# Two blocks on one NeuronCore: the order of VectorE's work in the key and state-space stage, and small matmuls placed in more tiles of the array

## The chip, the cores and the metric

The kernel runs on one NeuronCore of one Trainium2 chip. The number is the time of one execution on the device in microseconds (us), less being better. The program is written by hand for five engines: TensorE multiplies matrices, VectorE and ScalarE work on rows of 128 partitions, GpSimd and SyncE start transfers. Each engine executes its own list of instructions strictly in the order in which it is written, and waits at semaphores for the others.

## The reference

Two transformer blocks with a sequence of 512 and a width of 1024, batch 1, all in float32. The change lies in the first of them:

```python
ssm_u, ssm_z, q, k, v, attn_z, q_idx, k_idx, w_idx = jnp.split(h @ w_in[l], split_points, axis=-1)
# state-space mixer: 32 groups of 16 channels, 64 complex states in each
bu = jnp.einsum('gpc,bsgc->bsgp', b_bar, ug)
_, states = lax.associative_scan(_ssm_combine, (a_seq, bu), axis=1)
y = jnp.einsum('gcp,bsgp->bsgc', c_mat, states).real + d_skip * uf
z = jax.nn.gelu(y); z = z * jax.nn.sigmoid(z @ w_glu + b_glu)
# sparse attention: 8 heads of 64, every query keeps its 128 best keys
k = rms_norm(k.reshape(bsz, seq, N_HEADS, HEAD_DIM), k_gain)
score = jnp.einsum('bqh,bqhs->bqs', wib, jax.nn.relu(rel))
_, sel = lax.top_k(score, 128)
p = jax.nn.softmax(jnp.einsum('bqhd,bqkhd->bqhk', qb, k_sel) * scale + bias)
```

The second block (retention, gated linear attention, window attention, feed-forward) is the longer part of the time and is not touched.

## The kernel before

Large products are computed in float32 precision from two fp32r parts: every weight tile (1024 x 256) is loaded by SyncE, ScalarE casts it to its high part (`split_high`, L1211), VectorE subtracts to get the low part (`split_low`, L1852), and TensorE does three matmuls for each 128 rows (`gemm_half`). A tile is two halves; a half takes 24 matmuls of 512 columns, or 48 of 256 for the value tiles. `w_low` is the semaphore that says that a tile's low part is there.

The stage of the change comes after the query tiles. TensorE's list is: second half of the first key tile; `key_stats` (sums of squares of the keys by head); `output_strip(0)`; the two halves of the second key tile and the halves of the first value tile, with a `key_stats` and an `output_strip` behind each of the first three; the first half of the second value tile; four matmuls that spread the inverse norms of the keys over partitions (`kr_psum`); the last value half; two small products for the gate; the 16 steps of state-space outputs (`y_psum`); transposes; the GLU product; and then the attention's logits, which need the keys, the values, and `z_ready`, `mod_ready` and `copied_dve`, the last of VectorE's signals in this stage.

`output_strip` computes, for each of 16 pairs j of groups and each of the two groups r in it, a strip of 16 x 128 numbers from the state matrices: contraction over 64 rows, 16 output rows. Four pairs make a strip q. ScalarE copies strip q out of PSUM with `strip_copy(q)` in two instructions. VectorE adds the skip term to all strips (`diag`, L2170), which needs the semaphore `strip_act` at 8, that is all four copies; GpSimd then spreads them into `toep` with eight DMAs, which TensorE's outputs read.

ScalarE's list here is: `head_chunk` (copy and square of a quarter of the keys, behind the half that computed it), `strip_copy(0)`, the cast of the first value tile, the third head chunk, `strip_copy(1)`, the fourth head chunk, `strip_copy(2)`, the cast of the second value tile, `strip_copy(3)`, the root of the key sums.

VectorE has three kinds of work: the low parts of the weights; `states(0)` and `states(1)`, each the rotations and scans of half of the pairs; and the selection of keys. `select_keys(n)` is n rounds, each of which finds the 8 largest scores of a row (L2095) and strikes them out (L2096). 48 rounds are needed, 16 for each of three query tiles, on 256, 384 and 512 scores; they may lie anywhere before the attention reads the masks, so the program spreads them by hand.

Of the kernel before, what the change touches and what calls it, by code (L numbers as in the profile page):

```python
# [19 lines left out]
P = 128  # L20
# [9 lines left out]
STEPS = 8  # L30
# [131 lines left out]
def hybrid_blocks(nc, wstream, xT, vecs, consts, head_rows, onehot, rel_bias, ssm_vec, ssm_b, ssm_c, d_skip,  # L162
# [13 lines left out]
    with ctx:  # L176
# [124 lines left out]
        cl_zero, bias_spread = sem("cl_zero"), sem("bias_spread")  # L301
        ki_copied, ki_doubled, wi_ready, wi_row, wi_psum, mod_row, gate_row = sem("ki_copied"), sem("ki_doubled"), sem("wi_ready"), sem("wi_row"), sem("wi_psum"), sem("mod_row"), sem("gate_row")
# [250 lines left out]
        def _(pe):  # L553
# [207 lines left out]
            def key_stats(c):  # L761

                s0 = SQ0["k"]
                pe.wait_ge(sq_ready, s0 + c + 1)
                mm(bank[3][0:HEADS, :], head_cols[:, c, :], sqb[:, (s0 + c) % 2, :], c == 0, c == 3)\
                    .then_inc(sq_used, 1)
# [33 lines left out]
            def output_strip(q):  # L800

                if q:
                    pe.wait_ge(strip_act, 2 * q)
                for i in range(4):
                    j = 4 * q + i
                    for r in range(2):
                        rows = slice(64 * r, 64 * r + 64)
                        out = bank[5 + r][0:GCH, i * P:i * P + P]
                        mm(out, bb_re[rows, j, :], cl_re[rows, j, 0:P], True, False)
                        ins = mm(out, bb_im[rows, j, :], cl_im[rows, j, 0:P], False, True)  # L810
                ins.then_inc(strip_psum, 1)
# [3 lines left out]
            output_strip(0)  # L815
# [3 lines left out]
            output_strip(1)  # L819
            gemm_half(gr, 1, "fm", h_hi, h_lo)  # L820
            key_stats(2)
            output_strip(2)
            gemm_half(G["v"][0], 0, "tm", h_hi, h_lo)
            key_stats(3)
            output_strip(3)
            gemm_half(G["v"][0], 1, "tm", h_hi, h_lo)
            gemm_half(G["v"][1], 0, "tm", h_hi, h_lo)
            pe.wait_ge(rstd_ready, ROOT["k"] + 1)
# [13 lines left out]
            for q in range(4):  # L842
                if q >= 2:
                    pe.wait_ge(y_act, 2 * q - 2)
                for i in range(4):
                    j = 4 * q + i
                    outs = [bank[4 + 2 * (q % 2) + r][0:64, i * P:i * P + P] for r in range(2)]
# [345 lines left out]
        def _(act):  # L1193
# [175 lines left out]
            def strip_copy(q):  # L1369

                act.wait_ge(strip_psum, q + 1)
                for r in range(2):
                    act.copy(strip[:, 8 * q + r:8 * q + 8:2, :],
                             bank[5 + r][0:GCH, :].rearrange("p (i c) -> p i c", c=P)).then_inc(strip_act, 1)
# [11 lines left out]
            act.activation(root[0:HEADS, :], bank[3][0:HEADS, :], ACT.Sqrt, bias=eps[0:HEADS, 0:1],  # L1386
                           scale=1.0 / 64).then_inc(root_ready, 1)
            for w, gr in enumerate(G["v"]):
                if w == 0:
                    evacuate_tm(gr, 0, v32[:, 0:2, 0:WC])  # L1390
                    evacuate_tm(gr, 1, v32[:, 2:4, 0:WC])
                    continue
# [1376 lines left out]
```

## Time and profile before

| | |
|---|---|
| Time, median of 3 runs | 1565.63 us (1564.47 to 1566.12) |
| The profiled execution: its own time | 1562.42 us |
| The profiled execution: span from first to last instruction | 1560.4 us |
| TensorE busy | 1489.6 us, 95% of the span |
| VectorE busy | 857.8 us, 55% |
| ScalarE busy | 601.4 us, 39% |
| Mean granted TensorE clock | 0.980 of full speed |

The span is one slice of the whole: the stage of the change lies between 158 and 271 us of it. A row of a timeline gives the start, the duration, the engine, the line of the program (a helper's, so many operations share L555 or L1809), what is written and read, how many instructions are merged in the row, and in brackets the idle time before it with what ended it. A float32 matmul appears as two instructions.

### The profile page before, as it was taken

To read this page: it belongs to the slowest core of one execution; us is meant where nothing else is said; L and a number is where in the kernel's file an instruction comes from. 1 tells how busy PE (TensorE), PEld (TensorE's weight loads), DVE (VectorE), ACT (ScalarE), POOL (GpSimd) and SP (SyncE) were. 2 spreads that over 40 slices of the span, in tenths; PEclk is the share of its full clock that TensorE was granted. 3 is DMA by queue.
4 is the path that set the end of the run, shared out by engine and by line. 5 is a ranking of instruction groups with operands and counts; after the bars stand their busy time and mean duration, and the time that the engine had idled before them with its cause. 6 is when DMAs were issued, how large, how long until landed. Compare 5 with 4: busy or idle time off the path is not lost.

```text
span 1560.4 us, 19534 instructions
## 1 busy us (share of the span) xinstructions
PE 1489.6 (95%) x7920; PEld 1196.7 (77%) x7920; DVE 857.8 (55%) x1445; ACT 601.4 (39%) x912; POOL 20.7 (1%) x36
## 2 busy tenths in 40 slices
PE   4799998999999999999999999999997999999997
PEld 1575786667887788888888877888886888888886
DVE  5889797785636664333426444433447644444234
ACT  3334515565324654333426434432333322222220
POOL 0011010000000000000000000000000000000000
PEclk8799999999999999999999999999998999999998
DMA  8523254105331211212222212222231232322221
GB/s 320 184 86 80 80 126 149 55 1 189 135 108 57 79 55 55 81 59 81 112 98 91 81 55 81 81 84 105 102 141 70 93 107 83 109 83 100 102 95 55
DMA packets 24472, 152.39 MB, mean 98 GB/s; under 512 B 3472, under 2 KB 6080, under 8 KB 8112
## 3 DMA queue, kind: packets, MB, share of 16 engines
q1 hardware_dynamic: 21872, 137.43, 24.3%
q0 software_dynamic: 2512, 13.72, 3.2%
q8 instruction: 63, 1.03, 0.3%
q14 instruction: 25, 0.20, 0.0%
HBM read 144.55 MB, written 7.88 MB: 98 GB/s over the span
## 4 chain that ended last, share of the span: by engine, by line
PE 86%; DVE 9%; ACT 2%; issue 1%; DMA 1%; SPq 0%; DVEq 0%; ACTq 0%
PE bank L555 84%; DVE score L2115 1%; DMA xr<-xT 1%; PE bank L962 1%; ACT w_hi L1211 1%; DVE score L2096 1%; DVE w_lo L1852 1%; DVE small L2095 1%; PE bank L894 0%; DVE sv L1809 0%; DVE rstd L1883 0%; DVE w_lo L1861 0%; DVE tval L2059 0%; DVE y_lo L1878 0%; DVE rstd L1924 0%
## 5 line engine op out<-in xcount | busy, mean ns | idle before, releaser
L555 PE MATMUL bank<-h_hi,w_hi 128*128 128x512 f32 (+1 forms) x1104 | 441.0, 399 | 12.6 <-DVE h_lo L2618 7.8
L555 PE MATMUL bank<-h_hi,w_lo 128*128 128x512 f32 (+1 forms) x1120 | 438.7, 392 | 0.0
L555 PE MATMUL bank<-h_lo,w_hi 128*128 128x512 f32 (+1 forms) x1104 | 432.2, 391 | 0.0
L1852 DVE TENSOR_TENSOR w_lo<-w_raw,w_hi 128x2048 fp32r<-128x2048 f32 (+2 forms) x106 | 239.2, 2257 | 256.9 <-ACT w_hi L1211 255.4
L555 PEld LDWEIGHTS bank<-h_hi,w_hi 128*128 128x128 f32 (+1 forms) x1104 | 208.1, 188 | 70.5 <-issue 22.2
L1211 ACT CAST w_hi<-w_raw 128x2048 fp32r<-128x2048 f32 (+2 forms) x109 | 204.5, 1876 | 138.7 <-PE bank L555 135.8
L555 PEld LDWEIGHTS bank<-h_hi,w_lo 128*128 128x128 f32 (+1 forms) x1120 | 211.1, 188 | 45.8 <-issue 0.9
L555 PEld LDWEIGHTS bank<-h_lo,w_hi 128*128 128x128 f32 (+1 forms) x1104 | 208.3, 189 | 42.4 <-issue 1.2
L555 PE MATMUL bank<-y_hi,w_hi 128*128 128x512 f32 x272 | 109.8, 404 | 4.6 <-DVE y_lo L1878 4.6
L555 PE MATMUL bank<-y_lo,w_hi 128*128 128x512 f32 x272 | 106.8, 393 | 0.0
L555 PE MATMUL bank<-y_hi,w_lo 128*128 128x512 f32 x272 | 106.8, 393 | 0.0
L555 PE MATMUL bank<-w_hi,h_hi 128*128 128x256 f32 x352 | 102.0, 290 | 0.0
L555 PE MATMUL bank<-w_hi,h_lo 128*128 128x256 f32 x352 | 100.3, 285 | 0.0
L555 PE MATMUL bank<-w_lo,h_hi 128*128 128x256 f32 x352 | 100.2, 285 | 0.0
L1558 ACT ACTIVATE sgb<-bank 128x512 f32<-128x512 f32 x40 | 23.9, 598 | 150.9 <-PE bank L555 150.9
L555 PE MATMUL bank<-f_hi,w_lo 128*128 128x512 f32 (+1 forms) x220 | 76.2, 347 | 0.0
L555 PEld LDWEIGHTS bank<-w_hi,h_hi 128*128 128x128 f32 x352 | 68.2, 194 | 7.3 <-issue 7.3
L555 PE MATMUL bank<-f_hi,w_hi 128*128 128x512 f32 (+1 forms) x196 | 69.7, 356 | 0.0
L555 PE MATMUL bank<-f_lo,w_hi 128*128 128x512 f32 (+1 forms) x196 | 69.4, 354 | 0.0
L555 PEld LDWEIGHTS bank<-w_lo,h_hi 128*128 128x128 f32 x352 | 68.2, 194 | 0.0
L555 PEld LDWEIGHTS bank<-w_hi,h_lo 128*128 128x128 f32 x352 | 68.2, 194 | 0.0
L555 PEld LDWEIGHTS bank<-y_hi,w_hi 128*128 128x128 f32 x272 | 51.6, 190 | 18.9 <-issue 5.7
(382 smaller groups left out, 1826.3 us busy)
## 6 DMA issues: line engine op xcount, KB each, us to landing
w_raw<-wstream SPq DMA_DIRECT2D x120, 1024.0 KB, 4.8
xr<-xT SPq DMA_DIRECT2D x2, 2048.0 KB, 11.1
w_raw<-wstream SPq DMA_DIRECT2D x4, 768.0 KB, 4.1
bias_rows<-bias_table POOLq DMA_DIRECT2D x1, 2560.0 KB, 12.2
bias<-bias_rows POOLq DMA_DIRECT2D x1, 2048.0 KB, 11.9
x_saved<-xr POOLq DMA_DIRECT2D x1, 2048.0 KB, 9.9
xr<-x_saved POOLq DMA_DIRECT2D x1, 2048.0 KB, 8.0
outT<-down SPq DMA_DIRECT2D x16, 128.0 KB, 1.8
```

The costliest lines, as they stand in the source:

```text
L555: return pe.matmul(out, lhsT, rhs, start=start, stop=stop)
L962: ins = pe.transpose(bank[ST_BANKS[t % 2]][:, j * P:j * P + P], lg[:, n % 2, j, kb * P:kb * P + P], ident)
L1211: act.copy(hi_of(s)[:, 0:kt, :], w_raw[:, i % RAW_SLOTS, 0:kt, :]).then_inc(w_high, 1)
L1558: act.activation(sgb[:, m % 2, :], bank[bk][:, :], func).then_inc(bank_free[bk], 1)
L1852: dve.tensor_tensor(w_low_of(s)[:, 0:kt, :], w_raw[:, i % RAW_SLOTS, 0:kt, :], hi_of(s)[:, 0:kt, :].bitcast(f32), ALU.subtract).then_inc(w ...
L2095: settle(dve.max(m8, s))
L2096: settle(dve.match_replace(s, m8, s, NEG_TAKEN))
L2115: dve.scalar_tensor_tensor(out=score[:, qt, 0:w], in0=sgb[:, i % 2, 0:w], scalar=wi[:, qt, h:h + 1], in1=score[:, qt, 0:w], op0=ALU.mult, ...
```

## The change

- `output_strip(q)`, four calls, becomes `output_strips()`, one call behind the first `key_stats`: strip q goes to PSUM partitions 32q to 32q + 15, so that the four q and the two r use eight tiles of the array; the loop over q and r is inside. `strip_copy(q)` stays where it was in ScalarE's list and waits for the one signal.
- The state-space outputs of group r go to PSUM partitions 64r to 64r + 63 (before, 0 to 63 for both).
- `key_stats` computes the sums by tokens: 128 partitions of tokens by 2 heads, four small matmuls for each quarter, as the queries' sums already are. ScalarE's root and VectorE's reciprocal then work on 128 x 32 instead of 8 x 512. A new `key_rows()` on TensorE transposes the result to 8 x 512 before the second value tile, and ScalarE copies it out (`kr_row`).
- On VectorE, six rounds stand before the wait for the query roots, none before `states(0)`; the skip term on the strips stands before `states(1)` instead of behind it; the 8 rounds behind `states(1)` are gone; the reciprocal of the key roots comes right behind `states(1)`, then the low part of the second value tile, then 5 rounds. Further on it is 12, 8 and three times 3 rounds instead of 14, 9 and three times 1. The number of rounds is 48 in both.

```diff
             def key_stats(c):
                 s0 = SQ0["k"]
                 pe.wait_ge(sq_ready, s0 + c + 1)
-                mm(bank[3][0:HEADS, :], head_cols[:, c, :], sqb[:, (s0 + c) % 2, :], c == 0, c == 3)\
-                    .then_inc(sq_used, 1)
+                for t in range(TT):
+                    ins = mm(bank[3][:, t * HEADS + 2 * c:t * HEADS + 2 * c + 2],
+                             sqb[:, (s0 + c) % 2, t * P:t * P + P], head_ones[:, 0:P:64], True, True)
+                ins.then_inc(sq_used, 1)
+
+            def key_rows():
+                pe.wait_ge(rstd_ready, ROOT["k"] + 1)
+                for t in range(TT):
+                    ins = pe.transpose(bank[3][0:HEADS, t * P:t * P + P], stat[:, 0, t * HEADS:(t + 1) * HEADS], ident)
+                ins.then_inc(kr_turned, 1)
...
-            def output_strip(q):
-                if q:
-                    pe.wait_ge(strip_act, 2 * q)
+            def output_strips():
                 for i in range(4):
-                    j = 4 * q + i
-                    for r in range(2):
-                        rows = slice(64 * r, 64 * r + 64)
-                        out = bank[5 + r][0:GCH, i * P:i * P + P]
-                        mm(out, bb_re[rows, j, :], cl_re[rows, j, 0:P], True, False)
-                        ins = mm(out, bb_im[rows, j, :], cl_im[rows, j, 0:P], False, True)
+                    for part in range(2):
+                        bb, cl = ((bb_re, cl_re), (bb_im, cl_im))[part]
+                        for q in range(4):
+                            for r in range(2):
+                                rows = slice(64 * r, 64 * r + 64)
+                                out = bank[5 + r][32 * q:32 * q + GCH, i * P:i * P + P]
+                                ins = mm(out, bb[rows, 4 * q + i, :], cl[rows, 4 * q + i, 0:P], part == 0, part == 1)
                 ins.then_inc(strip_psum, 1)
...
-            output_strip(0)
+            output_strips()
             gr = G["k"][1]
             gemm_half(gr, 0, "fm", h_hi, h_lo)
             key_stats(1)
-            output_strip(1)
             gemm_half(gr, 1, "fm", h_hi, h_lo)
             key_stats(2)
-            output_strip(2)
             gemm_half(G["v"][0], 0, "tm", h_hi, h_lo)
             key_stats(3)
-            output_strip(3)
             gemm_half(G["v"][0], 1, "tm", h_hi, h_lo)
+            key_rows()
             gemm_half(G["v"][1], 0, "tm", h_hi, h_lo)
-            pe.wait_ge(rstd_ready, ROOT["k"] + 1)
+            pe.wait_ge(kr_row, 1)
...
-                    outs = [bank[4 + 2 * (q % 2) + r][0:64, i * P:i * P + P] for r in range(2)]
+                    outs = [bank[4 + 2 * (q % 2) + r][64 * r:64 * r + 64, i * P:i * P + P] for r in range(2)]
...
             stt(qg[:, :], v("q_gain", 0), -0.125, v("k_gain", 0), ALU.mult, ALU.mult)
+            select_keys(6)
             dve.wait_ge(root_ready, ROOT["q"] + 1)
...
             split_low(8)
-            select_keys(4)
             states(0)
             split_low(9)
-            states(1)
-            settle(dve.memset(ga_[:, :, 0:1], 0.0))
-            dve.memset(gb_[:, :, 0:1], 0.0).then_inc(state_ready, 1)
-            select_keys(8)
-            split_low(10)
             dve.wait_ge(strip_act, 8)
...
             dve.wait_ge(strip_ready, 1)
+            states(1)
+            settle(dve.memset(ga_[:, :, 0:1], 0.0))
+            dve.memset(gb_[:, :, 0:1], 0.0).then_inc(state_ready, 1)
             dve.wait_ge(root_ready, ROOT["k"] + 1)
-            dve.reciprocal(rstd[0:HEADS, :], root[0:HEADS, :]).then_inc(rstd_ready, 1)
-            select_keys(2)
+            dve.reciprocal(stat[:, 0, :], stat[:, 0, :]).then_inc(rstd_ready, 1)
+            split_low(10)
+            select_keys(5)
...
-            select_keys(14)
+            select_keys(12)
             split_low(G["glu"][0].s)
-            select_keys(9)
+            select_keys(8)
...
                     if m < 3:
-                        select_keys(1)
+                        select_keys(3)
```

On VectorE, around the skip term of the strips (`strip<-strip,tval`; `w_lo` is a low part, MAX and MATCH_REPLACE a round), the kernel before has:

```order
L2095 MAX small<-score 128x8 [waits dve_step]
L2096 MATCH_REPLACE score<-small,score 128x256 [waits dve_step]
L1852 TENSOR_TENSOR w_lo<-w_raw,w_hi 128x2048 [waits w_high,dve_step]
L1809 TENSOR_TENSOR tval<-cst,small 16x512 [waits strip_act]
L2170 TENSOR_TENSOR strip<-strip,tval 16x32x16 [waits dve_step]
L2173 RECIPROCAL rstd<-root 8x512 [waits root_ready,strip_ready]
```

and the changed kernel has, behind the first half of the states (`gb_`) and before the second (`tval<-ga_,cos_t`):

```order
L1818 TENSOR_TENSOR gb_<-gb_,tval 128x8x63 [waits dve_step]
L1861 TENSOR_TENSOR w_lo<-w_raw,w_hi 128x2048 [waits w_high,dve_step]
L1818 TENSOR_TENSOR tval<-cst,small 16x512 [waits strip_act]
L2174 TENSOR_TENSOR strip<-strip,tval 16x32x16 [waits dve_step]
L1818 TENSOR_TENSOR tval<-ga_,cos_t 128x512 [waits x_act,strip_ready]
L1818 TENSOR_TENSOR tval<-gb_,sin_t 128x512 [waits dve_step]
```

The instruction that waits for `strip_act` has moved ahead of `states(1)` and of the rounds, and everything of VectorE that follows is queued behind it.

Behind the second half of the states, the changed kernel has on VectorE:

```order
L1818 TENSOR_TENSOR gb_<-gb_,tval 128x8x63 [waits dve_step]
L2177 MEMSET ga_ 128x16 [waits dve_step]
L2178 MEMSET gb_ 128x16 [waits dve_step]
L2180 RECIPROCAL stat<-stat 128x32 [waits root_ready]
L1861 TENSOR_TENSOR w_lo<-w_raw,w_hi 128x2048 [waits w_high]
L2104 MAX small<-score 128x8
L2105 MATCH_REPLACE score<-small,score 128x256 [waits dve_step]
```

The reciprocal of the key roots, now on 128 x 32, and the low part of the second value tile stand directly behind `states(1)`; before, 8 rounds lay between.

On TensorE, the strips (`bb_re`, `bb_im` with `cl_re`, `cl_im`) behind the first sums of the keys read, before:

```order
L555 MATMUL bank<-h_hi,w_lo 128x512
L555 MATMUL bank<-sqb,cst 8x512
L555 MATMUL bank<-cl_re,bb_re 16x128
L555 MATMUL bank<-cl_im,bb_im 16x128
L555 MATMUL bank<-cl_re,bb_re 16x128
```

and now:

```order
L556 MATMUL bank<-h_hi,w_lo 128x512
L556 MATMUL bank<-cst,sqb 128x2 x4
L556 MATMUL bank<-cl_re,bb_re 16x128 x8
L556 MATMUL bank<-cl_im,bb_im 16x128 x8
L556 MATMUL bank<-cl_re,bb_re 16x128 x8
```

The real parts of all eight tiles of an i come first, then the imaginary ones, and the strips no longer alternate with key and value tiles.

Later on TensorE, between the two value tiles, there is now:

```order
L556 MATMUL bank1<-w_hi,h_lo 128x256
L775 MATMUL bank3<-cst,stat 8x128 [waits rstd_ready]
L775 MATMUL bank3<-cst,stat 8x128 x3
L556 MATMUL bank2<-w_hi,h_hi 128x256 [waits w_low,bank_free2]
L556 MATMUL bank2<-w_lo,h_hi 128x256
```

The transposes of the key roots (`cst,stat`) wait for VectorE's reciprocal, and the value tile behind them (`w_hi,h_hi` into bank 2) for its low part; nothing of TensorE's list can pass them.

## Rows read from the trace of the kernel before

**Rows 1.** The page, part 4: shares of the span on the chain that ended last

```profile
PE 86%; DVE 9%; ACT 2%; issue 1%; DMA 1%; SPq 0%; DVEq 0%; ACTq 0%
```

**Rows 2.** Timeline of VectorE, 163 to 184: start us, us, operation, [idle before]

```profile
163.89 0.35 DVE L2131 RECIPROCAL stat<-stat 128x32 f32<-128x32 f32 x1 [5.33 <-ACT stat L1357]
...
167.82 0.42 DVE L2095 MAX8 small<-score 128x8 f32<-128x256 f32 x1
...
168.79 0.43 DVE L2095 MAX8 small<-score 128x8 f32<-128x256 f32 x1
...
171.74 0.69 DVE L1809 TENSOR_TENSOR tval<-ga_,cos_t 128x512 f32<-128x512 f32 x1
...
183.47 2.29 DVE L1852 TENSOR_TENSOR w_lo<-w_raw,w_hi 128x2048 fp32r<-128x2048 f32 x1
```

**Rows 3.** Timeline of TensorE, 174 to 183, first strip and the half behind it

```profile
174.48 0.40 PE L555 MATMUL bank<-cl_re,bb_re 64*16 64x128 f32 x4
...
176.34 0.50 PE L555 MATMUL bank<-h_hi,w_hi 128*128 128x512 f32 x1
...
182.02 1.02 PE L555 MATMUL bank<-sqb,cst 128*8 128x512 f32 x2
```

**Rows 4.** TensorE's groups by form, 163 to 250: xcount | busy us, mean ns

```profile
L555 PE MATMUL bank<-ut,win_re 128*64 128x64 f32 x64 | 2.3, 223 | 0.5 <-ACT stat L1357 0.5
```

**Rows 5.** Timeline of ScalarE, 191 to 204

```profile
191.23 0.60 ACT L1225 ACTIVATE sqb<-bank 128x512 f32<-128x512 f32 x1
...
194.41 1.91 ACT L1211 CAST w_hi<-w_raw 128x2048 fp32r<-128x2048 f32 x1
...
202.21 1.05 ACT L1373 COPY strip<-bank 16x512 f32<-16x512 f32 x2 [5.90 <-PE bank L555]
```

**Rows 6.** Timeline of VectorE, 207 to 215, strips, key roots, keys

```profile
207.63 0.67 DVE L1809 TENSOR_TENSOR tval<-cst,small 16x512 f32<-16x512 f32 x1
...
209.04 3.34 DVE L2173 RECIPROCAL rstd<-root 8x512 f32<-8x512 f32 x1
...
215.03 3.25 DVE L2177 SCALAR_TENSOR_TENSOR k<-k,qg,bank 128x512 f32<-128x512 f32 x4 [0.29 <-PE bank L555]
```

**Rows 7.** Timeline of TensorE, 207 to 228: last value tile, start of the outputs

```profile
207.95 0.28 PE L555 MATMUL bank<-w_hi,h_hi 128*128 128x256 f32 x1
...
213.80 3.70 PE L555 MATMUL bank<-rstd,sgb 8*128 8x512 f32 x8
...
226.74 0.43 PE L555 MATMUL bank<-cl_re,ga_ 64*64 64x128 f32 x4
...
227.32 0.65 PE L555 MATMUL bank<-toep,ut 128*64 128x128 f32 x4
...
227.90 0.43 PE L555 MATMUL bank<-cl_re,ga_ 64*64 64x128 f32 x4
```

**Rows 8.** Timeline of VectorE, 238 to 256

```profile
238.27 1.23 DVE L1852 TENSOR_TENSOR w_lo<-w_raw,w_hi 128x1024 fp32r<-128x1024 f32 x1 [2.49 <-ACT w_hi L1211]
...
242.30 0.69 DVE L2095 MAX8 small<-score 128x8 f32<-128x512 f32 x1
...
243.81 0.69 DVE L2095 MAX8 small<-score 128x8 f32<-128x512 f32 x1
...
253.06 2.50 DVE L1878 TENSOR_TENSOR y_lo<-z,y_hi 128x512 fp32r<-128x512 f32 x4 [0.17 <-DVE score L2096]
```

**Rows 9.** Timeline of TensorE, the three longest waits in question

```profile
253.90 0.77 PE L555 MATMUL bank<-y_hi,w_hi 128*128 128x512 f32 x1 [3.10 <-DVE y_lo L1878]
...
270.56 0.49 PE L555 MATMUL bank<-k,q 64*128 64x128 f32 x4 [2.29 <-DVEq L2201]
...
1181.75 0.77 PE L555 MATMUL bank<-h_hi,w_hi 128*128 128x512 f32 x1 [7.82 <-DVE h_lo L2618]
...
1187.01 0.47 PE L555 MATMUL bank<-h_hi,w_hi 128*128 128x512 f32 x1
```

**Rows 10.** Windows: PE busy, PEld, DVE, ACT, POOL, then the granted clock

```profile
1182.00:1186.00 4.00, 4.00 (x10) 3.17 (x11) 3.93 (x7) 2.38 (x5) 0.00 (x0) 0.50 0.00 0
```

More of the change, by code:

```diff
@@ L301, in hybrid_blocks @@
         cl_zero, bias_spread = sem("cl_zero"), sem("bias_spread")
+        kr_turned, kr_row = sem("kr_turned"), sem("kr_row")
         ki_copied, ki_doubled, wi_ready, wi_row, wi_psum, mod_row, gate_row = sem("ki_copied"), sem("ki_doubled"), sem("wi_ready"), sem("wi_row"), sem("wi_psum"), sem("mod_row"), sem("gate_row")
@@ L1369, in strip_copy @@
             def strip_copy(q):
-                act.wait_ge(strip_psum, q + 1)
+                act.wait_ge(strip_psum, 1)
                 for r in range(2):
                     act.copy(strip[:, 8 * q + r:8 * q + 8:2, :],
-                             bank[5 + r][0:GCH, :].rearrange("p (i c) -> p i c", c=P)).then_inc(strip_act, 1)
+                             bank[5 + r][32 * q:32 * q + GCH, :].rearrange("p (i c) -> p i c", c=P)).then_inc(strip_act, 1)
             strip_copy(0)
@@ L1385, in _ @@
             act.wait_ge(rstd_ready, ROOT["k"])
-            act.activation(root[0:HEADS, :], bank[3][0:HEADS, :], ACT.Sqrt, bias=eps[0:HEADS, 0:1],
+            act.activation(stat[:, 0, :], bank[3][:, 0:32], ACT.Sqrt, bias=eps[:, 0:1],
                            scale=1.0 / 64).then_inc(root_ready, 1)
@@ L1391, in _ @@
                     evacuate_tm(gr, 1, v32[:, 2:4, 0:WC])
+                    act.wait_ge(kr_turned, 1)
+                    act.copy(rstd[0:HEADS, :], bank[3][0:HEADS, :]).then_inc(kr_row, 1)
                     continue
@@ L1413, in _ @@
                              u[:, :, 128 * q:128 * q + 128].rearrange("p t (i c) -> p i t c", c=GCH)[:, 1:8:2, :, :],
-                             bank[4 + 2 * (q % 2) + r][0:64, :].rearrange("p (i t c) -> p i t c", i=4, t=STEPS))\
+                             bank[4 + 2 * (q % 2) + r][64 * r:64 * r + 64, :].rearrange("p (i t c) -> p i t c", i=4, t=STEPS))\
                        .then_inc(y_act, 1)
```

## The prediction

> **What bounds the kernel now.** I read first the chain of work that ended last: 86% of the span is TensorE's own work [rows 1]. A change pays here only if it takes work off TensorE, or a wait of TensorE, and it costs whatever TensorE newly waits. Then I read the waits of TensorE in the stage of the change, 158 to 271 us: it waits for VectorE twice, 3.10 us ahead of the GLU product and 2.29 us ahead of the logits [rows 9], since VectorE finishes its rounds late. So VectorE's list sets when the stage ends, and TensorE's list is dense beside it. Last I read the three timelines, to see who hands what to whom when the lists are written anew. All times below are on the clock of the profiled execution.
>
> **The head of VectorE's list.** Six rounds now fill the wait of 5.33 us ahead of the query roots. A round on 256 scores takes 168.79 - 167.82 = 0.97 us [rows 2], six take 5.8, so the roots are late by 0.5 us, and nobody needs them then. `states(0)`, which started at 171.74 behind four rounds, can start at 167.9, when ScalarE has copied its input. It takes 183.47 - 171.74 = 11.7 us [rows 2] and ends at 179.6. So far VectorE is 3.9 us ahead.
>
> **Strips on TensorE.** A strip takes 176.34 - 174.48 = 1.86 us [rows 3], four take 7.4. Now the 128 instructions lie on eight array tiles instead of two. If all eight run side by side, they take a quarter, 1.9 us. From the other side, 64 instructions of 64 columns on two tiles took 2.3 us [rows 4], 36 ns each; if instructions can't follow each other faster than that, 128 take 4.6. I take 2.7, nearer to the first because that row has the shorter columns but four times the weights to load. The page "TensorE: Matmul & The Clock Gate" of the Trainium skill has two rules that disagree here. Its section on the measured speedup of packing gives a pack the time of one matmul and about 4 ns per tile more, which makes an estimate of 2.3 us; its section "Wait — 56ns, not 53.3ns?" says that two matmuls never start closer than about 25 ns, an estimate of 3.2 us. By the first the sum below is 0.4 us less, by the second 0.5 more. No row here has eight tiles.
>
> With 2.7 the first key half behind the strips starts at 177.2 (before 176.34). A half takes 182.02 - 176.34 = 5.7 us [rows 3]. The sums of the keys take 1.0 in both forms, so I cost that edit at nothing. The second key half then ends at 177.2 + 5.7 + 1.0 + 5.7 = 189.6.
>
> **The wait that the change adds.** VectorE now has the skip term, and with it the wait for all four strip copies, ahead of `states(1)`. The copies don't follow the strips. ScalarE's list has the fourth head chunk, the third strip copy and a cast ahead of the last one. The chunk needs the second key half, 189.6; copy and square 1.3 (the square 0.60, the copy about the same); strip copy 1.05; cast 1.91; strip copy 1.05 [rows 5]: 195.0. VectorE has done its low part by about 182.3 and stands still for 12.7 us. The rounds that used to lie here are now late. The skip term takes 209.04 - 207.63 = 1.4 us [rows 6], to 196.4, `states(1)` 11.7, to 208.1. The reciprocal takes 0.35, as one of the same form did [rows 2], instead of 3.34 us [rows 6], which is the change's clear gain on VectorE, 3.0 us, and ends at 208.6. The low part behind it ends at 210.8 (2.2 us to the next instruction).
>
> TensorE has had nothing since 189.6 + 1.0 + 5.9 + 1.0 + 5.9 = 203.4. A value half is 213.80 - 207.95 = 5.9 [rows 7]. The transposes wait until 208.6 and take 0.9; the value tile waits for its low part until 210.9. In the kernel before it began at 207.95 [rows 7]. TensorE is 3.0 us late, in spite of 4.7 us saved on strips.
>
> **The granted clock.** TensorE has waited 6.6 us in two pieces. After the wait of 7.82 us at 1181.75 twelve matmuls of 512 columns took 1187.01 - 1181.75 = 5.3 us [rows 9] at a granted clock of 0.50 [rows 10], the level of 1.2 GHz; at full clock they take 2.8, so such a wait costs 2.5 more. After the one of 3.10 us the first matmul took 0.77 too, and after 2.29 us nothing was lost (0.49) [rows 9]. I take 1.5 us here, as the transposes bear part of it, bounds 0 and 2.5. The shift is 4.5 us.
>
> **From the keys to the GLU.** The keys end at 215.03 + 3.25 + 4.5 = 222.8 [rows 6], the outputs start at 226.74 + 4.5 = 231.2 [rows 7]. The transfers into `toep` started 13 us earlier and are no issue. Now an output step: 227.90 - 226.74 = 1.16 us, of which the products with `toep` take 0.58, two one behind the other in the same array columns [rows 7]. In different columns they can run together. That takes at most half, 0.29; I take 0.21, to 0.95 per step, since each step also changes the shape of the tiles twice. The bounds are 0.87 and 1.16. VectorE does 12 rounds, three of 0.97, nine on 384 scores of 1.24 (midway to 1.51 for 512, 243.81 - 242.30 [rows 8]), and a mask of 0.5: to 237.4. It waits for the GLU tile's cast, which ScalarE has behind the eighth output step: 231.2 + 8 x 0.95, and 2.2 us of copy and cast as before (226.74 + 8 x 1.16 + 2.2 = 238.2, the row at 238.27), gives 241.0. Low part 1.2, then seven rounds of 1.24, a mask, one of 1.51: 252.9. In the kernel before VectorE was there at 253.06 [rows 8], so it looks even. But by then it has done 33 rounds, and before it had done 39.
>
> **The end of the stage.** The six missing rounds come between the GLU's gates. From 253.06 to the logits at 270.56 [rows 8, 9] VectorE had 2.5 of `y_lo`, two low parts (1.2 and 2.2), four products of 0.75 (0.69 as the first instruction of the states [rows 2], and the step to the next), three rounds of 1.51: 13.4 of work and 4.1 of waits. Now 9.1 more of rounds cover most of the waits, of which I keep 1.8. So 13.4 + 9.1 + 1.8 = 24.3, and the logits start at 277.2: 6.6 us late. TensorE's GLU ends near 268, so it waits about 9 us ahead of the logits, and there the half clock costs its full 2.5 us [rows 9, 10]. The attention behind has TensorE in the chain, which keeps both.
>
> The sum: 3.0 late at the value tile, 1.5 clock, 2.1 more by late rounds and the cast, 2.5 clock: 9.1 us. On the execution's own time, 1562.4 + 9.1 = 1571.5; it lay 3.2 below the median of the runs, so the median is 1565.6 + 9.1 = 1574.7.
>
> The tiling page of the Trainium skill ("TensorEngine Tiling (Array Packing)", section "PSUM Bottleneck") warns that packing doesn't speed up the evacuation, which then may become the bottleneck. By it alone four copies of 1.05 us behind the strips would end at 181.4 and hold nobody. Here the copies' place in ScalarE's list costs 13 us more than their duration, so I go by the list.
>
> **The rivals.**
> Tiles don't run together. If the eight tiles and the two column halves run no faster than before, strips cost 4.7 more, and the outputs delay the cast by 1.7 and the gelu by as much again: 9.1 + 4.7 + 3.4 = 17.2, time 1582.8. Against it speaks that two tiles do share the array now: 32 instructions of 128 columns in 1.86 us are 58 ns each, while two of 512 columns take 1.02 us, so one of 128 about 120 ns [rows 3]. Chance 5%.
>
> No half clock. If the clock stays up at both waits, it is 5.1, and 3.7 with strips of 1.9 and steps of 0.87: 1569.3 to 1570.7. For it speaks only the wait of 2.29 us; both waits here are far longer. Inside my range, as part of the forecast.
>
> The wait for the strips is short. If ScalarE's copies come long before 195, say by 182 as the bare durations allow, `states(1)` starts 12.7 us sooner, the roots are there before TensorE asks, the value tile starts at 204.2, 3.8 us earlier than before, and VectorE waits for TensorE's keys and for the cast instead. By the same steps the keys end at 214.5, the outputs start at 223, the rounds end at 245, the logits start at 269: 1.6 us early. With a half clock ahead of the logits it is 0.9 late, no change: 1566; chance 12%, where I count also a forecast that falls short by two terms. Without it, and with both tile gains at their best, it is 3.8 us early: 1561.8, faster, chance 6%. It decides at the strip copies: VectorE's wait there must be under about 1 us for this. Against it stands the list of ScalarE, which the change leaves as it is.
>
> **How the numbers follow.** Forecast as summed, with its own bounds, 77%; the tiles' rival 5%; no change 12%; faster 6%. A measurement of this kernel tells 0.2%, 3.1 us, from no change. Ends of the forecast: strips 1.9 (-0.8), steps 0.87 (-0.6), no clock loss at the value tile (-1.5), half of the last (-1.2), gives 5.0: 1570.6; strips 4.6 (+1.9), steps 1.16 (+3.4) give 1580. The range takes in the no-change case in part: 1566.5 to 1578.5. Slower 0.82, same 0.12, faster 0.06.
>
> **What would show it.** In the changed profile: VectorE idle for 12 to 13 us ahead of the skip term, ended by a strip copy of ScalarE; TensorE idle for 5 us ahead of the transposes and for 8 to 9 ahead of the logits, ended by VectorE; a granted clock of about 0.5 behind the latter; strips in about 2.7 us; output steps of 0.95. I am wrong if the skip term runs before 185, or if the second value tile starts before 208.

## The result and the profile after

The changed kernel takes 1573.8 us (median, 1572.7 to 1575.6), the kernel before 1565.9 on the same chip: a ratio of 1.0056, 95% interval 1.004 to 1.0071. It is slower by about 8 us. The execution that left the trace took 1575.6, with a span of 1573.7. The page, its busy times and the shares of the chain:

```profile
PE 1491.0 (95%) x7948; PEld 1199.0 (76%) x7948; DVE 854.7 (54%) x1445; ACT 602.1 (38%) x913; POOL 20.7 (1%) x36
...
PE 85%; DVE 10%; ACT 2%; issue 1%; DMA 1%; SPq 0%; DVEq 0%; ACTq 0%
```

VectorE's share of the chain is a point higher than in [rows 1] and TensorE's a point lower. VectorE has 3.1 us less work than before (857.8), but TensorE is busy 1.4 us longer (1489.6 before), although the tiles take some 9 us of matmuls off it: its matmuls run at a lower clock for longer. The traced span is 13.3 us longer than before, more than the medians differ. I cut it at two marks that all kernels here have: ScalarE's root of the query sums, and the first logits on TensorE.

| us | before | after | difference |
|---|---|---|---|
| start to the root of the query sums | 163.5 | 167.3 | +3.8 |
| from there to the first logits | 107.1 | 114.9 | +7.8 |
| logits to the end | 1289.8 | 1291.5 | +1.7 |

I count the first piece as no effect of the change. It lies between 163.1 and 167.5 us in the ten kernels of this text, and e6 and e7, whose lists up to there are those of before, have 166.4 and 166.6. What the change does is in the second piece and just behind it. The waits of TensorE from 150 to 430 us (sum, times, longest), of the four that VectorE ends and that stand in the stage:

```profile
PE bank L556 <- DVEq L2209: 10.1, 1, 10.1
PE bank L775 <- DVE stat L2180: 5.8, 1, 5.8
...
PE bank L556 <- DVE y_lo L1887: 2.3, 4, 0.8
PE bank L556 <- DVE w_lo L1861: 1.2, 1, 1.2
```

The longest waits of 3.10 and 2.29 us in [rows 9] have become 0.8 and 10.1, and 5.8 + 1.2 us are new. VectorE's timeline has their origin:

```profile
183.44 2.29 DVE L1861 TENSOR_TENSOR w_lo<-w_raw,w_hi 128x2048 fp32r<-128x2048 f32 x1
197.54 0.68 DVE L1818 TENSOR_TENSOR tval<-cst,small 16x512 f32<-16x512 f32 x1 [11.81 <-ACT strip L1380]
...
210.86 0.33 DVE L2180 RECIPROCAL stat<-stat 128x32 f32<-128x32 f32 x1
...
211.11 2.23 DVE L1861 TENSOR_TENSOR w_lo<-w_raw,w_hi 128x2048 fp32r<-128x2048 f32 x1
```

VectorE is through with its low part at about 185.7 and then stands still for 11.8 us; `states(1)`, the reciprocal and the low part of the value tile stand behind. ScalarE's timeline of the same stretch, to be read beside [rows 5]:

```profile
193.55 1.06 ACT L1380 COPY strip<-bank 16x512 f32<-16x512 f32 x2
194.52 1.90 ACT L1218 CAST w_hi<-w_raw 128x2048 fp32r<-128x2048 f32 x1
196.44 1.06 ACT L1380 COPY strip<-bank 16x512 f32<-16x512 f32 x2
```

All strips had been in PSUM since 180, and each copy takes 1.06 us. But the last one stands behind the fourth head chunk and a cast of 1.90. On TensorE the strips (first, second and last of eight rows, and the key half behind them) against [rows 3]:

```profile
178.10 0.44 PE L556 MATMUL bank<-cl_re,bb_re 64*16 64x128 f32 x16
178.33 0.42 PE L556 MATMUL bank<-cl_im,bb_im 64*16 64x128 f32 x16
...
179.64 0.46 PE L556 MATMUL bank<-cl_im,bb_im 64*16 64x128 f32 x16
180.03 0.50 PE L556 MATMUL bank<-h_hi,w_hi 128*128 128x512 f32 x1
```

The rows of 16 instructions start about 0.22 us apart, 14 ns each. From the first strip to the key half behind them it is 180.03 - 178.10 = 1.93 us for all four strips, where one took 1.86 by the same count. TensorE then waits on the transposes and again on the value tile, against [rows 7]:

```profile
211.25 1.02 PE L775 MATMUL bank<-cst,stat 128*8 128x128 f32 x4 [5.77 <-DVE stat L2180]
213.48 0.55 PE L556 MATMUL bank<-w_hi,h_hi 128*128 128x256 f32 x1 [1.22 <-DVE w_lo L1861]
...
217.25 0.36 PE L556 MATMUL bank<-w_hi,h_lo 128*128 128x256 f32 x1
```

Up to 217.25 the value tile's matmuls start 0.21 us apart, then 0.12. The windows show the same (third number from the end: the granted clock):

```profile
213.40:217.40 4.00, 3.92 (x18) 3.95 (x19) 3.72 (x13) 0.00 (x0) 0.00 (x0) 0.50 0.68 225
217.40:221.10 3.70, 3.70 (x32) 3.60 (x30) 0.70 (x3) 0.00 (x0) 0.00 (x0) 1.00 0.00 0
...
225.50:230.80 5.30, 5.30 (x26) 5.30 (x27) 4.96 (x15) 0.00 (x0) 0.00 (x0) 0.50 0.00 0
```

The same tile in the kernel before ran its first half at 1.00, and only a part of the second lower:

```profile
207.90:213.80 5.90, 5.90 (x51) 5.77 (x50) 5.73 (x9) 0.59 (x1) 4.47 (x8) 1.00 0.82 224
...
218.00:221.50 3.50, 3.50 (x19) 3.50 (x19) 3.29 (x10) 0.00 (x0) 0.00 (x0) 0.55 0.97 87
```

The output steps, whose distance was 1.16 [rows 7], stand 0.96 apart:

```profile
233.72 1.93 PE L556 MATMUL bank<-w_raw,silu_g 128*32 128x256 f32 x32
235.58 0.43 PE L556 MATMUL bank<-cl_re,ga_ 64*64 64x128 f32 x4
...
236.54 0.44 PE L556 MATMUL bank<-cl_re,ga_ 64*64 64x128 f32 x4
```

Last, the first and the second logits. Before they are 6.1 us apart, the first at 270.56 [rows 9] and the second here:

```profile
276.65 0.49 PE L555 MATMUL bank<-k,q 64*128 64x128 f32 x4
```

Now they are 7.7 apart, with the window behind the first:

```profile
282.20 0.80 PE L556 MATMUL bank<-k,q 64*128 64x128 f32 x4 [10.13 <-DVEq L2209]
...
289.89 0.38 PE L556 MATMUL bank<-k,q 64*128 64x128 f32 x2
```

```profile
282.20:287.00 4.80, 4.80 (x16) 3.77 (x17) 1.87 (x9) 2.78 (x5) 0.00 (x0) 0.64 0.00 2
```

### The profile page after: what moved, and what is told of

It reads as the page before. It is cut to its first block, busy times and chain, and to the rows that moved or that the text cites. A ratio compares the mean times of both kernels' runs of the same rounds, so it can differ in the third digit from the quotient of the medians.

```text
span 1573.7 us, 19589 instructions
## 1 busy us (share of the span) xinstructions
PE 1491.0 (95%) x7948; PEld 1199.0 (76%) x7948; DVE 854.7 (54%) x1445; ACT 602.1 (38%) x913; POOL 20.7 (1%) x36
## 4 chain that ended last, share of the span: by engine, by line
PE 85%; DVE 10%; ACT 2%; issue 1%; DMA 1%; SPq 0%; DVEq 0%; ACTq 0%
PE bank L556 83%; DVE score L2124 1%; DMA xr<-xT 1%; PE bank L969 1%; DVE score L2105 1%; DVE w_lo L1861 1%; DVE small L2104 1%; ACT w_hi L1218 1%; DVE tval L1818 1%; PE bank L901 0%; DVE sv L1818 0%; DVE rstd L1892 0%; DVE w_lo L1870 0%; DVE tval L2068 0%; DVE y_lo L1887 0%
```

## The experiments

The eight kernels were timed beside the kernel before, twelve runs of each and six of e5; the changed one was timed ahead of them, in four runs. "Stage" is the time from the root of the query sums to the first logits, and it is 107.1 before and 114.9 after.

| kernel | median us | ratio to before, 95% | stage us | TensorE's wait ahead of the logits |
|---|---|---|---|---|
| changed kernel | 1573.8 | 1.0056 (1.0040 to 1.0071) | 114.9 | 10.1 |
| skip term later (e1) | 1566.2 | 1.0001 (0.9988 to 1.0014) | 102.4 | 9.2 |
| wait filled with rounds (e2) | 1564.8 | 0.9995 (0.9981 to 1.0008) | 106.4 | 2.0 |
| strip copies earlier (e3) | 1564.8 | 0.9999 (0.9984 to 1.0013) | 102.4 | 9.2 |
| before, tile places alone (e4) | 1566.7 | 1.0007 (0.9994 to 1.0019) | 107.4 | 2.3 |
| e1 with the rounds spread (e5) | 1557.1 | 0.9943 (0.9928 to 0.9959) | 99.8 | 2.3 |
| before, key norms by tokens alone (e6) | 1568.2 | 1.0017 (1.0005 to 1.0030) | 109.9 | 2.3 |
| e4 with the low half first (e7) | 1566.8 | 1.0007 (0.9995 to 1.0020) | 107.3 | 2.3 |
| e5 without the tile places (e8) | 1563.6 | 0.9989 (0.9977 to 1.0000) | 106.1 | 2.3 |

My theory: what the change loses is VectorE's wait for the last strip copy and what stands behind it. Rivals: that the rounds in the GLU alone cost the time, that the half clock does, or that the new forms (tiles, tokens) are dearer than the old. For the clock it helps to look at one more stretch in each trace: from the first of the eight products with 8 rows that spread the key norms (`rstd,sgb`) to the end of the second value tile. The work in it is the same in every kernel. It took 11.1 us before and in e4 and e8, 12.6 in the changed kernel, e2 and e5, 12.7 in e6, 15.0 in e7, and 9.6 in e1 and e3, where alone the clock did not fall.

**e1, the skip term behind `states(1)`.**

```diff
             split_low(9)
+            states(1)
+            settle(dve.memset(ga_[:, :, 0:1], 0.0))
+            dve.memset(gb_[:, :, 0:1], 0.0).then_inc(state_ready, 1)
             dve.wait_ge(strip_act, 8)
             diag = flat[0:GCH, 0:GROUPS * GCH].rearrange("p (g c) -> p g c", c=GCH)
...
             dve.wait_ge(strip_ready, 1)
-            states(1)
-            settle(dve.memset(ga_[:, :, 0:1], 0.0))
-            dve.memset(gb_[:, :, 0:1], 0.0).then_inc(state_ready, 1)
```

> The changed kernel with the skip term on the strips, and its wait for the strip copies, put back behind states(1). Theory: the wait of 11.8 us is what the change loses. VectorE runs states(1) at once, the wait shrinks to under 0.5 us, the value tile starts when TensorE is free (7 us sooner), the keys and the outputs follow 10 us sooner, and the logits start about 11.7 us sooner than in the changed kernel. TensorE then still waits about 10 us ahead of the logits, since nine rounds lie between the gates, so its half clock there stays. Time 1564 us, 10 below the changed kernel and 2 below the one before. Rival: the loss is the rounds that were put off to the GLU's gates, and the wait is absorbed behind the outputs; then this kernel is no faster than the changed one, 1573 us.

VectorE's timeline, from the start of `states(1)`:

```profile
184.67 0.69 DVE L1818 TENSOR_TENSOR tval<-ga_,cos_t 128x512 f32<-128x512 f32 x1
...
196.59 0.68 DVE L1818 TENSOR_TENSOR tval<-cst,small 16x512 f32<-16x512 f32 x1
...
199.11 0.36 DVE L2180 RECIPROCAL stat<-stat 128x32 f32<-128x32 f32 x1 [1.12 <-ACT stat L1393]
...
211.87 0.75 DVE L2185 SCALAR_TENSOR_TENSOR k<-k,qg,bank 128x512 f32<-128x512 f32 x1 [5.48 <-PE bank L556]
```

`states(1)` follows at once, the strip wait is gone, the reciprocal of the roots starts at 199.1 (210.9 after), and TensorE waits neither for it nor for the low half. The stage is 12.5 us shorter than in the changed kernel. Counted from the query root, the products of the key norms start 9.5 us earlier. The other 3.0 are the clock behind them: it stayed at full speed from there to the end of the tile, 9.6 us instead of 12.6.

```profile
210.60:220.20 9.60, 9.60 (x57) 7.22 (x56) 7.72 (x18) 0.79 (x2) 0.00 (x0) 1.00 0.49 125
```

That these 3.0 belong to the wait isn't shown, since e5 has no such wait either and has the lower clock there (below). The median gains 7.6 us on the changed kernel's. VectorE still has nine rounds left for the GLU, so TensorE waits 9.2 us ahead of the logits and the first ones run at the lower level again:

```profile
268.69 0.80 PE L556 MATMUL bank<-k,q 64*128 64x128 f32 x4 [9.25 <-DVEq L2209]
```

Those four took 0.49 before [rows 9]. From the logits on, this run needs 3.5 us more than the kernel before, 2.5 of it by the second logits, and 1.8 more than the changed one. The rest comes 555 us later, in the second block, where this trace has 3 us at the lower clock and the kernel before has none:

```profile
823.70:826.70 3.00, 3.00 (x16) 3.00 (x16) 2.84 (x2) 2.94 (x4) 0.00 (x0) 0.50 0.66 273
```

That is part of why 12.5 us of stage come out as 7.6 in the medians (9.0 in e3). Another part is that the traced executions are single ones: the changed kernel's lies 1.8 us above its median, e1's 2.4 below its own.

**e3, the same wait removed on ScalarE.**

```diff
             strip_copy(0)
             ahead(G["k"][1])
+            for q in range(1, 4):
+                strip_copy(q)
             head_chunk("k", 2, k32)
-            strip_copy(1)
             head_chunk("k", 3, k32)
-            strip_copy(2)
             ahead(G["v"][0])
-            strip_copy(3)
```

> The changed kernel with ScalarE's strip copies 1 to 3 directly behind the cast of the first value tile instead of one behind each head chunk and cast. Theory: what holds VectorE is the place of the copies in ScalarE's list and not their duration; with the copies done about 186.5 us (in the changed profile's time) VectorE waits under 1.5 us instead of 11.8. The rest as with the skip term behind states(1): value tile 7 us sooner, logits 10 to 12 sooner, time 1564 us. By the rival theory (rounds between the gates) 1573 us. If copies were held by PSUM or by their duration, the wait would stay above 5 us.

ScalarE's timeline:

```profile
177.20 1.05 ACT L1380 COPY strip<-bank 16x512 f32<-16x512 f32 x2 [1.54 <-PE bank L556]
178.16 1.91 ACT L1218 CAST w_hi<-w_raw 128x2048 fp32r<-128x2048 f32 x1
180.09 3.23 ACT L1380 COPY strip<-bank 16x512 f32<-16x512 f32 x6
183.35 0.59 ACT L1348 COPY k<-bank 128x512 f32<-128x512 f32 x1
```

The six copies end 19.0 us behind the root of the query sums (183.3), in the changed kernel 30.2 (197.5). VectorE's order is that of the changed kernel, and yet key roots, keys, outputs, GLU and logits come within 0.02 us of where e1 has them, counted from the root of the query sums. Two edits on two engines that share nothing but this wait give the same stage. The wait is the cause, and nothing else in the new place of the skip term shows in the stage.

**e2, eleven rounds in the wait, none in the GLU.**

```diff
             split_low(9)
+            select_keys(11)
             dve.wait_ge(strip_act, 8)
...
-            select_keys(8)
+            select_keys(6)
...
-                        select_keys(3)
+                        select_keys(0)
```

> The changed kernel with 11 rounds put into the wait for the strip copies, none between the GLU's gates, and 6 instead of 8 ahead of the GLU's input; 48 in all. The wait itself and the late value tile stay. Theory (VectorE's list ends the stage): the logits no longer wait for rounds, but for the GLU product; they start about 12 us sooner than in the changed kernel, about 4 sooner than before, and the half clock ahead of them goes. The value tile's lateness of 3 us with its half clock stays. Time 1561.5 us. Rival (the loss is the late value tile and TensorE's clock there): then only the logits' own wait shrinks partly, and the time stays above 1568.

TensorE's waits from 150 to 300 us:

```profile
PE bank L775 <- DVE stat L2181: 5.8, 1, 5.8
...
PE bank L556 <- DVEq L2210: 2.0, 1, 2.0
PE bank L556 <- DVE w_lo L1861: 1.2, 1, 1.2
```

The late roots stay, 5.8 + 1.2 us with the half clock behind, and still 8.5 us of stage are regained, at the same clock up to the end of the value tile as in the changed kernel, since VectorE is on time at the logits. I expected 1561.5. The reason: even without rounds the stretch from `y_lo` to the logits takes 17.7 us against 17.5 before, so TensorE and ScalarE bound it. It can't make up for a late GLU; it can only be spared nine rounds, with which it takes 24.7.

So the same 8 us can be had at either end: on time at the value tile, with a wait ahead of the logits, or the reverse. e5 does both.

**e4, the kernel before with the tile places alone.**

```diff
-            def output_strip(q):
+            def output_strips():
...
-                        out = bank[5 + r][0:GCH, i * P:i * P + P]
+                                out = bank[5 + r][32 * q:32 * q + GCH, i * P:i * P + P]
...
-                    outs = [bank[4 + 2 * (q % 2) + r][0:64, i * P:i * P + P] for r in range(2)]
+                    outs = [bank[4 + 2 * (q % 2) + r][64 * r:64 * r + 64, i * P:i * P + P] for r in range(2)]
```

> The kernel before with only the new places in the array: the strips in eight tiles in one call, the outputs of the two groups in different columns. VectorE's list is that of before. Theory: strips take 1.8 us instead of 7.4 and an output step 0.95 instead of 1.16, 9 us off TensorE, but VectorE's list ends the stage, and TensorE only waits longer for it. VectorE gains at most its wait of 2.5 us for the GLU tile's cast. Time 1564.5 us, between 1562 and 1567. Rival: TensorE's list counts in full here, time 1557 us.

TensorE's waits from 150 to 300 us:

```profile
PE bank L555 <- DVE w_lo L1848: 5.3, 1, 5.3
PE bank L555 <- DVE y_lo L1874: 4.8, 1, 4.8
```

The strips take 5.5 us less and the outputs about 3, and the kernel is not faster (1.0007). Most of it stands again as waits for VectorE: 5.3 for the low half, which the eight rounds hold up, 4.8 instead of 3.1 ahead of the GLU. Another part went to the clock: behind the wait of 5.3 the first half of the value tile ran at the lower level, and from the tile's start to its end it takes 19.6 us, 16.9 before. This rules out that the tiles themselves are dear.

**e7, e4 with the low half ahead of the eight rounds.**

```diff
-            select_keys(8)
             split_low(10)
+            select_keys(8)
```

> e4_tiles_only with the low part of the second value tile ahead of the 8 rounds instead of behind them. In e4_tiles_only TensorE reached that tile 5.3 us sooner and waited 5.3 us for its low part. Theory: with the low part early this wait goes, the keys come 2.9 us sooner (VectorE no longer waits for them), the stage takes 104.5 us instead of 107.4, time 1563.5 us. Rival: VectorE's list is what it is, and nothing changes: 1566.5 us.

```profile
PE bank L555 <- DVE rstd L2169: 4.1, 1, 4.1
```

The wait for the low half is gone, and one of 4.1 for the key roots stands in its place, since the rounds now stand ahead of the reciprocal alone. The keys do come 2.9 us sooner than in e4, as expected. But behind the wait of 4.1 the eight products with 8 rows took 7.2 us instead of 3.7 in e4, all at a granted clock of 0.50, and from them to the end of the tile it takes 15.0 us instead of 11.1. The tile ends where e4 ends it (63.9 and 64.0 us behind the query root), so nothing is gained (1.0007).

**e6, the kernel before with the key norms by tokens alone.**

```diff
+                for t in range(TT):
+                    ins = mm(bank[3][:, t * HEADS + 2 * c:t * HEADS + 2 * c + 2],
+                             sqb[:, (s0 + c) % 2, t * P:t * P + P], head_ones[:, 0:P:64], True, True)
...
+            key_rows()
+            pe.wait_ge(kr_row, 1)
...
-            dve.reciprocal(rstd[0:HEADS, :], root[0:HEADS, :]).then_inc(rstd_ready, 1)
+            dve.reciprocal(stat[:, 0, :], stat[:, 0, :]).then_inc(rstd_ready, 1)
```

> The kernel before with the key norms by tokens alone (sums on 128 x 2, root and reciprocal on 128 x 32, transposes directly ahead of the matmuls that spread the norms, and ScalarE's copy behind them). Theory: VectorE saves 3.0 us on the reciprocal, but it then waits for the keys, as transposes, copy and semaphores put about 2 us between the value half and the spread; the keys come 1.7 us later than before, and so does the rest: 1567.5 us. The gain exists only where the transposes have run earlier. Rival: the 3.0 us count in full, 1563 us.

```profile
216.60 0.60 PE L775 MATMUL bank<-cst,stat 128*8 128x128 f32 x4
218.10 3.73 PE L556 MATMUL bank<-rstd,sgb 8*128 8x512 f32 x6 [0.90 <-ACT rstd L1407]
```

VectorE's reciprocal is 3 us shorter, but the transposes and ScalarE's copy now stand between a value half and the keys (216.60 to 218.10), and the reciprocal wasn't what TensorE waited for. It costs 0.17% (0.05 to 0.3), 2.8 us of stage. The products of the key norms start 1.4 us later than before, and from them to the end of the tile it takes 12.7 us instead of 11.1, so about half of the loss is the clock. In the changed kernel the transposes stand ahead of a value half, which covers ScalarE's copy (212.36, 0.57 us).

**e5, e1 with the rounds spread.** The rounds per place are 6, then 9 behind the low half, 14 behind the keys, 8, and one between the GLU's gates.

```diff
-            select_keys(5)
+            select_keys(9)
...
-            select_keys(12)
+            select_keys(14)
...
-                        select_keys(3)
+                        select_keys(1)
```

> e1_diag_late with the rounds spread where VectorE still waits in it: 6 at the head, 9 instead of 5 ahead of the keys (it waited 5.5 us there), 14 instead of 12 behind them (2.4 us), 8, and 1 instead of 3 between the GLU's gates. Theory: VectorE's idle time in the stage is what separates it from the other kernels; with about 8 us of it filled, the stage from the query roots to the logits takes 96 to 97 us, against 107.1 before and 102.4 in e1_diag_late, and TensorE's wait of 9.2 us ahead of the logits falls to about 2.3, so that the half clock behind it (second logits 8.5 instead of 6.1 us after the first) goes as well. Time 1555.5 us, 10 below the kernel before. Rival: the attention behind takes back what is gained, as it took 3.4 us back in e1_diag_late for reasons other than the clock; then 1560 or more.

TensorE's waits from 150 to 300 us, and the first logits:

```profile
PE bank L556 <- DVE y_lo L1887: 3.5, 1, 3.5
...
PE bank L556 <- DVEq L2209: 2.3, 1, 2.3
```

```profile
262.88 0.49 PE L556 MATMUL bank<-k,q 64*128 64x128 f32 x4 [2.29 <-DVEq L2209]
```

1557.1 us: 0.57% faster than the kernel before (0.41 to 0.72). It lies 1.1% under the changed kernel's median, which was measured at another time, so without an interval. The logits take 0.49 again, and from there to the end it needs 1289.8, as the kernel before does. I expected a stage of 96 to 97 and got 99.8. A part of the miss is the clock. The products of the key norms start 44.3 us behind the query root, as in e1, but behind them TensorE runs at the lower level, and the tile ends 3.0 us later than in e1:

```profile
210.40:216.80 6.40, 6.40 (x24) 4.89 (x24) 5.20 (x12) 0.00 (x0) 0.00 (x0) 0.50 0.32 88
```

VectorE waits 1.57 us for the GLU tile's cast, which stands behind it, so I estimate that about 1.6 of the 3.0 reached the stage. What is left is 3.5 us ahead of the GLU and VectorE's idle time:

```profile
231.89 1.23 DVE L1861 TENSOR_TENSOR w_lo<-w_raw,w_hi 128x1024 fp32r<-128x1024 f32 x1 [1.57 <-ACT w_hi L1218]
...
252.33 0.69 DVE L1818 TENSOR_TENSOR z<-sgb,z 128x512 f32<-128x512 f32 x1 [1.88 <-ACTq L1446]
...
257.12 2.29 DVE L1861 TENSOR_TENSOR w_lo<-w_raw,w_hi 128x2048 fp32r<-128x2048 f32 x1 [1.35 <-ACT w_hi L1218]
```

In these and one more place (0.42 us, at 255.08) VectorE waits for a gate or a cast, while rounds are still to be done: with rounds of 1.5 us, spare pieces of 0.4 to 1.9 us can't be filled without some loss.

**e8, e5 with the array places of before.**

```diff
-            output_strips()
+            output_strip(0)
...
-                    outs = [bank[4 + 2 * (q % 2) + r][64 * r:64 * r + 64, i * P:i * P + P] for r in range(2)]
+                    outs = [bank[4 + 2 * (q % 2) + r][0:64, i * P:i * P + P] for r in range(2)]
```

> e5_spread with strips and outputs in the array places of the kernel before, VectorE's list unchanged. Theory: once VectorE's list is filled, TensorE's 9 us count: the keys come 5.6 us later, the cast for the GLU tile 9, VectorE waits again by as much, and the stage takes about 106 us: time 1565 us, 9.5 above e5_spread. Rival: the tiles don't matter even then, since VectorE's work alone ends the stage; then within 3 us of e5_spread.

VectorE's longest wait, from 160 to 290 us:

```profile
DVE tval L1822 <- ACT strip L1384: 8.8, 1, 8.8
```

1563.6. The same edit, worth nothing in e4, is worth 6.6 us here (difference of the medians; no run of the one overlaps the other), where I expected 9.5. By the traces the stage differs by 6.3, although e5 lost 1.6 us more than e8 to the clock behind the key norms. Part is TensorE's own time, part is that strips made one by one behind key and value halves are copied late, so that the skip term waits 8.8 us even behind `states(1)`. How the 6.6 divide between the two wasn't tried, so they are the price of places and single call together.

## Why the prediction was right

The forecast was 1574.7 and the median is 1573.8; the path was mostly the one foreseen. That the number came out within 1 us is partly luck: four terms of 3.0, 1.5, 2.1 and 2.5 us measured 1.7, 3.3, 2.8 and 1.7, and the errors cancel.

- **Rounds at the head.** They cost nothing, as predicted. I had the query roots 0.5 late; with the root itself at 167.3, VectorE even waits 1.1 us for it. In e5, where it comes at 163.1, they are 0.6 late.
- **Strips.** 1.93 us, not 2.7: the lower bound of 1.9. Of the two rules weighed, the packing rule of the Trainium skill's page "TensorE: Matmul & The Clock Gate" (its section on the measured speedup of packing) gave 2.3, and the floor of 25 ns (section "Wait — 56ns, not 53.3ns?") 3.2; the trace has 14 ns per instruction and so contradicts the floor for tiles that run side by side. My reason for going above 1.9, four times the weights, was not borne out. The upper bound was also read too high: 36 ns is busy time with its overlaps, and by their starts those groups of 32 instructions stand 0.93 to 0.96 us apart, 30 ns each, which makes 3.8 us and not 4.6.
- **The wait for the strip copy.** 12.7 predicted, 11.8 measured; the reading of ScalarE's list held. The last copy ends at 197.5, which is 193.7 on the clock of the kernel before. e1 and e3 show that this wait carries the loss.
- **TensorE at the value tile.** Predicted: transposes 5.2 late, the value tile 1.4 more. Measured 5.77 and 1.22. The value tile starts at 213.48, or 209.7 on the clock of before, 1.7 later than there and not 3.0, as strips and wait were both shorter.
- **The half clock there.** This is the mis-sized term: 1.5 predicted. From the start of the value tile to the end of its second half it takes 20.2 us (213.48 to 233.72), before 16.9 (207.95 to 224.87), so 3.3; in e2, with the same waits, 20.3. The first half of the tile, behind the waits, took 7.7 us instead of 5.8: 1.8 of the 3.3, near the 1.5 that I took. The other 1.5 came in the second half, behind the 8-row products of the keys, where the kernel before runs at the lower level for a shorter time; the prediction had no term for it. No run ties it to the change: e5 has the long stretch without a wait ahead of it, e1 and e3 have none. With the start 1.3 less late, the two errors nearly cancel: 5.0 behind at the end of the tile, where the sum had 4.5.
- **Output steps** 0.96 against 0.95 predicted, 1.16 before.
- **GLU and logits.** `y_lo` comes 90.2 behind the query root, before 89.6: nearly even, as predicted, with six rounds fewer done. From there to the logits 24.7 us (24.3 predicted), the logits 7.8 late (6.6 predicted), TensorE's wait 10.1 (about 9). e2, which takes the rounds out of this stretch, puts the logits 8.5 us earlier: the term of the late rounds is shown.
- **The half clock behind the logits.** 2.5 predicted. The second logits come 1.6 later than before; in e1 and e3, with waits of 9.2, 2.5 later. Behind the changed kernel's logits the granted clock is 0.64 over 4.8 us, so it rose within them; in e1 it rose 5.4 us behind the first logits, in the changed kernel 3.5 (from windows of 1 us).
- **Sum.** 9.1 predicted; the stage and the part behind it in the trace give 7.8 + 1.7 = 9.5, the medians 8. The stated range stopped at 1578.5, below the 1580 of the prediction's own upper ends.

The rival "tiles don't run together" is refuted by 1.93 us for four strips, "no half clock" by the windows. "The wait for the strips is short" was false for the change, but e1 and e3 make its condition true, and then its forecast can be checked: it said logits 1.6 early, then 0.9 late by the clock, 1566. The logits are 4.7 early, the part behind gives 3.5 back, and the times are 1566.2 and 1564.8. The time was right, but the step to the logits was underrated by 3 us, 1.5 of it because the clock didn't fall behind the key norms as it does before, and the part behind by 1. Its bracket "faster at 1561.8" didn't come, since the half clock came each time the wait was long.

The clock also moved the times where the change doesn't reach. Where the part behind the logits is 0.8 to 1.2 us longer than the second logits account for (e1, e2, e3, e4, e6, e7), each trace has a stretch at the lower clock that the kernel before doesn't have there, about 207 us behind the logits in e2, e3 and e6 and about 554 us behind them in e1, e4 and e7. It costs 1.4 to 1.6 us, and differences of at most 0.9 elsewhere make up the rest. All of it lies where the programs are the same.

What stays open: why the clock fell at these places in some executions and not in others, and above all why it stayed up behind the key norms in e1 and e3 alone, which is worth 3.0 us against e5. I have one trace of each kernel, so I can't say how often it does either.

## What to carry to other kernels

A wait is to be priced by the place that its releaser has in the other engine's list, and not by how long the releaser takes: four copies of 1.06 us held VectorE 11.8 us, and moving either the wait or the copies gave back 12.5 us of the stage, 9.5 of them apart from the clock behind the key norms. Time taken off the busiest engine gains only if those who feed it are early: the same edit (tile places and one call for the strips) gained nothing in a list where VectorE was late, and 6.6 us where it was on time. Work that can go anywhere, such as the rounds, belongs where its engine would wait, with few in the stretch just ahead of the point for which the busiest engine waits; and a wait of several microseconds removed from TensorE can be worth more than its length, since matmuls behind it may run at the lower level. Single differences of 1 to 3 us between two traces are to be held against the granted clock before a cause is given for them.

## What the runs showed of the hardware

- Matmuls on eight array tiles (64 rows by 16 used columns, 128 columns of data) started 14 ns apart, and the next product came 1.93 us behind the first of the 128, against 58 ns on two tiles. The products were ordered so that all eight tiles take the real part and then all eight the imaginary part, and they still ran side by side.
- The same wait came with either level of the clock. The logits behind a wait of 2.29 took 0.49 and came at full clock before [rows 9], in e5 and in e8; in e4, e6 and e7, with the same wait of 2.29, the second logits come 7.7 us behind the first instead of 6.1, as they do behind long waits. At 159 us a wait of 2.28 was followed by the lower level in the changed kernel, and one of 2.30 wasn't before, in code that is the same. Ahead of the changed kernel's GLU product the wait was only 0.82, and the granted clock was 0.51 from 254.8 to 261.6 even so.
- TensorE busy is not TensorE at full clock: behind eight products with 8 rows (4.15 us, no idle time) the granted clock was 0.50 for 5.3 us in the changed kernel and 0.55 for 3.5 us in the one before. But it needn't fall there: in e1 it was 1.00 from the same products to the end of the tile.
- The shape of a reciprocal decides its price: 8x512 took 3.34 us [rows 6], the same 4,096 numbers as 128x32 took 0.33.
